# Norms by logarithm and exponential on ScalarE, and expert table units moved from the first down product to the second gate and up product

## What is computed

```
y = x * rsqrt(mean(x * x) + 1e-6) * gain
```

## Time and profile before

| | |
|---|---|
| runs of the kernel | 3768.0, 3773.07 and 3775.91 us, median 3773.07 |
| the profiled execution | 3776.11 us, span 3774.3 us |
| mean granted TensorE clock | 0.971 of full speed |
| TensorE matrix products busy | 3540.8 us, 94% of the span |
| VectorE busy | 2212.3 us, 59% |
| ScalarE busy | 1366.3 us, 36% |
| GpSimd busy | 1836.6 us, 49% |

### The profile page before, as it was taken

How to read it: one execution, slowest core, us unless ns; L and a number is a source line. 1 busy time by engine, 2 the same in 40 slices (tenths; PEclk the granted TensorE clock), 3 DMA queues, 4 the chain that set the end, 5 groups by cost and what they waited for, 6 DMA issues and landing times. The chain is left out here.

```text
span 3774.3 us, 49804 instructions
## 1 busy us (share of the span) xinstructions
PE 3540.8 (94%) x17547; PEld 2997.5 (79%) x17547; DVE 2212.3 (59%) x4244; ACT 1366.3 (36%) x1915; POOL 1836.6 (49%) x909
## 2 busy tenths in 40 slices
PE   8999987899999899996888999989999999999999
PEld 5777766777787688773677667769999999999999
DVE  4553255422234355216675565458999998677776
ACT  4332234233344322222323245423335454444443
POOL 5666423223344254332333311335566666788886
PEclk9999988999999999997999999999999999999999
DMA  6997854444557266331324211586448999899996
GB/s 244 382 375 262 301 165 149 130 137 151 160 192 245 67 201 190 105 107 39 125 88 133 88 57 62 184 302 224 158 162 295 347 344 348 317 397 389 384 383 237
DMA packets 458130, 813.81 MB, mean 216 GB/s; under 512 B 31544, under 2 KB 308984, under 8 KB 455322
## 3 DMA queue, kind: packets, MB, share of 16 engines
q1 hardware_dynamic: 278416, 436.07, 34.4%
q10 hardware_dynamic: 142666, 241.11, 18.2%
q0 software_dynamic: 36864, 134.23, 9.4%
HBM read 682.84 MB, written 195.56 MB: 233 GB/s over the span
## 5 line engine op out<-in xcount | busy, mean ns | idle before, releaser
L536 POOL TENSOR_TENSOR weights_lo<-weights_raw,weights_hi 128x1024 fp32r<-128x1024 f32 x649 | 1591.6, 2457 | 1866.1 <-ACT weights_hi L1211 1743.8
L612 PE MATMUL bank<-operand_hi,weights_hi 128*128 128x512 f32 (+1 forms) x2856 | 1095.3, 384 | 65.4 <-DVE operand_lo L1904 24.2
L614 PE MATMUL bank<-operand_hi,weights_lo 128*128 128x512 f32 (+1 forms) x2856 | 1065.1, 373 | 0.0
L613 PE MATMUL bank<-operand_lo,weights_hi 128*128 128x512 f32 (+1 forms) x2856 | 1064.3, 373 | 0.0
L1211 ACT ACTIVATE weights_hi<-weights_raw 128x1024 fp32r<-128x1024 f32 x649 | 682.3, 1056 | 827.5 <-PE bank L614 649.0
L612 PEld LDWEIGHTS bank<-operand_hi,weights_hi 128*128 128x128 f32 x2856 | 542.4, 190 | 158.7 <-DVE operand_lo L1904 30.4
L613 PEld LDWEIGHTS bank<-operand_lo,weights_hi 128*128 128x128 f32 x2856 | 542.7, 190 | 75.2 <-issue 6.4
L614 PEld LDWEIGHTS bank<-operand_hi,weights_lo 128*128 128x128 f32 x2856 | 540.8, 189 | 75.1
L612 PE MATMUL bank<-expert_hi,weights_hi 128*128 128x384 f32 x1024 | 344.1, 336 | 0.0
L613 PE MATMUL bank<-expert_lo,weights_hi 128*128 128x384 f32 x1024 | 344.0, 336 | 0.0
L614 PE MATMUL bank<-expert_hi,weights_lo 128*128 128x384 f32 x1024 | 344.0, 336 | 0.0
(11 more groups left out here) (397 smaller groups left out, 4979.2 us busy)
## 6 DMA issues: line engine op xcount, KB each, us to landing
weights_raw<-in_w_ffn_gu SPq DMA_DIRECT2D x132, 512.0 KB, 5.8
expert_table_v<-in_w_peer_out SPq DMA_DIRECT2D x120, 512.0 KB, 5.4
weights_raw<-in_w_peer_ahead SPq DMA_DIRECT2D x120, 512.0 KB, 3.8
weights_raw<-in_w_peer_out SPq DMA_DIRECT2D x120, 512.0 KB, 6.4
expert_table_u<-expert_turned ACTq DMA_DIRECT2D x288, 128.0 KB, 4.6
expert_rows<-in_w_peer_ahead ACTq DMA_DIRECT2D x64, 512.0 KB, 6.7
peer_gates<-gate_stage SPq DMA_DIRECT2D x24, 1024.0 KB, 8.6
expert_gates<-peer_gates ACTq DMA_DIRECT2D x16, 1536.0 KB, 12.5
```

The costliest lines, as they stand in the source:

```text
L536: pool.tensor_tensor(LO[:, slot, :], RAW[:, slot, :], HI[:, slot, :].bitcast(F32), ALU.subtract).then_inc(sem("lo_ready"), 1)
L612: pe.matmul(out, wh, hi(k), start=(k == 0), stop=False)
L613: pe.matmul(out, wh, lo(k), start=False, stop=False)
L614: ins = pe.matmul(out, wl, hi(k), start=False, stop=(k == kc - 1))
```

## The change

A norm's first step and its reciprocal leave VectorE. ScalarE computes Ln of the scaled sum plus epsilon straight from the bank, then Exp of minus one half of it; where asked, it first loads the one table set that has both functions, before its waits. VectorE only waits. Six of the `d1` units stay (two each at blocks 1, 2 and 3), eighteen move to `f2`, which turns two per pair and saves them in the same pair, behind the SiLU. The wait for the `d1` stores moves behind the norm. Two norms get other destination buffers.

```
-TABLE = {"f1": range(0, 54), "d1": range(54, 78), "f2": range(78, 96), "q": range(96, 128)}
+TABLE = {"f1": range(0, 54), "d1": range(54, 60), "f2": range(60, 96), "q": range(96, 128)}
+DOWN_TURNS = [0, 2, 2, 2, 0, 0, 0, 0]
...
-            def root(width):
+            def root(width, denom=D, bank=4, out=None, read=None, table=True):
                 n["sum"] += 1
+                if table:
+                    act.preload_act_table_set("natural_log_exp_and_others")
+                act.wait_ge(sem("square_used"), n["square"])
+                act.activation(RT[:, 0:width], BANK[bank][:, 0:width], ACT.Ln, bias=TINY[:], scale=1.0 / denom)\
+                    .then_inc(sem("sum_read"), 1)
                 act.wait_ge(sem("sum_read"), n["sum"])
-                act.activation(RT[:, 0:width], MS[:, 0:width], ACT.Sqrt).then_inc(sem("root_ready"), 1)
+                if read:
+                    act.wait_ge(sem(read[0]), read[1])
+                act.activation(RSTD[:, 0:width] if out is None else out, RT[:, 0:width], ACT.Exp, scale=-0.5)\
+                    .then_inc(sem("root_ready"), 1)
...
-                        if s == 0 and 3 <= pair <= 20:
+                        if s == 0 and mix == 2 and 3 <= pair <= 20:
                             save_rows(which)
...
-                        if s >= 2 and 2 <= pair <= 19:
-                            save_rows(which)
+                        if 2 <= pair <= 19:
+                            if mix == 2 and s >= 2:
+                                save_rows(which)
+                            elif mix == 1 and s == 1:
+                                for _ in range(2):
+                                    save_rows(which)
...
                     if name == "ffn1":
-                        for _ in range(3):
+                        for _ in range(DOWN_TURNS[m]):
                             save_rows("d1")
                     square(YT[:, m, :], TOK, "block_free", n["freed"] + m + 1)
-                    if name == "ffn1" and m == DC - 1:
-                        for i in range(2):
-                            act.wait_ge(sem(f"table_stored_d1{i}"), 64 * len(TABLE["d1"]) // 2)
...
             ffn("ffn1", n["freed"], x_squares)
             root(TOK)
+            for i in range(2):
+                act.wait_ge(sem(f"table_stored_d1{i}"), 64 * len(TABLE["d1"]) // 2)
...
-                root(TOK)
+                root(TOK, P, read=("piece_made", n["f"] + h) if h else None, table=h == 0)
...
                 if c % 2:
-                    root(TOK)
+                    root(TOK, 64, out=MS[:] if c == 3 else None, table=c == 1)
...
             for c in range(8):
-                root(TOK)
+                root(TOK, 64, table=c == 0)
...
-            def rstd(pieces, denom, width, bank=4, out=None):
-                n["square"] += pieces
+            def rstd():
                 n["sum"] += 1
-                dve.wait_ge(sem("square_used"), n["square"])
-                dve.tensor_scalar(MS[:, 0:width], BANK[bank][:, 0:width], 1.0 / denom, EPS, ALU.mult, ALU.add)\
-                    .then_inc(sem("sum_read"), 1)
                 dve.wait_ge(sem("root_ready"), n["sum"])
-                link(dve.reciprocal(RSTD[:, 0:width] if out is None else out, RT[:, 0:width]))
...
-                which, each = ("f2", 1) if k else ("f1", 3)
+                which, each = ("f2", 2) if k else ("f1", 3)
...
                     for m in range(DC):
-                        for t in range(3 * m, 3 * m + 3):
+                        for t in range(sum(DOWN_TURNS[:m]), sum(DOWN_TURNS[:m + 1])):
                             turn_rows("d1", t)
                         copy_blocks(YT, 1, FC, first=m, scaled=True)
```

More of the change, by code:

```diff
@@ L169, in late_at @@
     return range(count * u // units, count * (u + 1) // units) if u < units else range(0)
-TABLE = {"f1": range(0, 54), "d1": range(54, 78), "f2": range(78, 96), "q": range(96, 128)}
+TABLE = {"f1": range(0, 54), "d1": range(54, 60), "f2": range(60, 96), "q": range(96, 128)}
+DOWN_TURNS = [0, 2, 2, 2, 0, 0, 0, 0]
+assert sum(DOWN_TURNS) == len(TABLE["d1"])
 WOUT_TURNS = 9
@@ L236, in program @@
         ms_at = fixed[0]
-        MS = place("mean_square", [P, TOK])
-        RT = place("root", [P, TOK])
+        MS = place("second_reciprocal_root", [P, TOK])
+        RT = place("log_mean_square", [P, TOK])
         RSTD = place("reciprocal_root", [P, TOK])
@@ L247, in program @@
         RSUM = place("exp_sum_reciprocal", [P, 2])
+        TINY = place("norm_epsilon", [P, 1])
         A0 = fixed[0]
@@ L1411, in ffn @@
                             square(CT[:, c, :], NMEM, "ctx_loaded", 16)
-                        root(NMEM)
+                        root(NMEM, bank=5, out=MS[:, NMEM:2 * NMEM])
                         highs(CXH, CT, DC, lambda c: MOD[:, c, 1:2])
@@ L1501, in x_squares @@
             def x_squares():
+                act.wait_ge(sem("epsilon_set"), 1)
                 for c in range(DC):
@@ L1852, in _ @@
             st = Stepper()
-            n = {"freed": 0, "square": 0, "sum": 0, "high": 0, "piece": 0, "exp": 0, "product": 0,
+            n = {"freed": 0, "sum": 0, "high": 0, "piece": 0, "exp": 0, "product": 0,
                  "gate": 0, "groups": [], "operand": 1, "made": 0}
             link = Link(dve, sem("dve_order"))
+            dve.memset(TINY[:], EPS).then_inc(sem("epsilon_set"), 1)
             def done(kc):
@@ L1981, in two_pairs @@
                             turn(i, p, 0)
-                            if each > 1:
-                                turn(i, p, 1)
+                            turn(i, p, 1)
                         dve.wait_ge(sem("pe_steps"), s0 + UNIT * ((2 * p + 1) * mix + 1) + 4 * mix * UNIT * i)
@@ L1992, in two_pairs @@
                                           ALU.subtract).then_inc(sem("hidden_ready"), 1)
-                        if table and each > 1:
+                        if table and each == 3:
                             turn(i, p, 2)
@@ L2013, in ffn @@
                     for m in range(DC):
-                        for t in range(3 * m, 3 * m + 3):
+                        for t in range(sum(DOWN_TURNS[:m]), sum(DOWN_TURNS[:m + 1])):
                             turn_rows("d1", t)
                         copy_blocks(YT, 1, FC, first=m, scaled=True)
-                    rstd(DC, D, TOK)
+                    rstd()
                 else:
                     copy_blocks(YT, 2, FC, scaled=True)
-                    n["square"] += 1
-                    rstd(DC, D, NMEM, 5, MS[:, NMEM:2 * NMEM])
+                    rstd()
                     normed(CT, CT, CXH, CXL, NMEM, lambda c: COEF[:, 1, c:c + 1], lambda c: MOD[:, c, 1:2],
@@ L2285, in _ @@
             for pair in range(2):
-                rstd(2, 64, TOK)
+                rstd()
+                by = MS if pair else RSTD
                 for j in range(2):
@@ L2307, in transformed @@
                 free(dve.tensor_tensor(KHAT[:, o, m, :], done(TT)[:], norm[:], ALU.mult))
-            for o, norm in enumerate((RSTD, RT)):
+            for o, norm in enumerate((RSTD, MS)):
                 dve.wait_ge(sem("abs_used"), 8 * (o + 1))
```

18 lines of the change are left out of this document (9 added, 9 removed).

## The result

The changed kernel took **3732.5 us** (median of 4 runs, 3727.2 to 3734.6) against 3774.5 for the kernel before on the same chip (3768.0 to 3778.4): ratio 0.989, 95% interval 0.987 to 0.991. The forecast was 3725 in a range of 3713 to 3740. The profiled execution took 3727.16 us, span 3725.3; before, 3776.11 and 3774.3: 49 us less, where the sum had said 48. By medians it is 42 us less, 6 short of the sum and 7.5 us above the time forecast, inside the range: the profiled execution was the fastest of the changed kernel's four.

What follows compares the result with a forecast made beforehand. The prediction took TensorE, at 94% of the span, as the bound. Gains from its shortened waits summed to 47.75, say 48 us, turning the median of 3773.07 us into 3725, range 3713 to 3740.

Steps and rivals of the forecast that it cites:

- First down product: First down product and its norm: three terms together take 15.6 us off the start of the next stage.
- (1): Start of the first down product: TensorE's wait for a low weight part goes, as block 0 saves none; 2.7 us.
- (2): End of the first down product: without units there, the last block is copied out sooner and the norm starts earlier; 8.2 us.
- (3): Norm behind the first down product: 3.35 us from the norm itself, plus its table load now beside the last sum; 4.7 us.
- Terms given back: Rival, chance 0.12: after a shortened wait VectorE or GpSimd is the next bound; gain 30 to 38 us, time 3740.
- Heads, output product, second projections: Exposed norms at the four heads, behind the output product and before the second block's projections: gains 3.9, 3.35 and 3.35 us.
- The first term: Behind the second down product: the norm's root ends earlier despite a new exposed table load; gain 1.4 us.
- The second term: Context keys: Ln frees the second sum's bank, which TensorE waited for, earlier; gain 2.0 us.
- Query and key norms: Eight norms in the second block: TensorE's work, not the norm chain, sets the swaps' pace at 7.35 us; gain 15.5 us.
- two loads per norm: Rival, chance 0.07: the preload doesn't hold, each Exp gets its own load, some 3 us in the query loop; time 3739.
- The moved units: 18 more units in the second gate and up product fit beside its matrix work; cost 0, bounds 0 to 9 us.
- the buffer loop: Second gate and up product: stores, load, landing and transpose must fit in a pair's 11.1 us, so landings may take 7.5.

Runs made afterwards that it cites:

- experiment 1: The change's two halves, each alone on the kernel before: new norms with old table-unit shares 3740.4 us; old norms with new shares 3757.5 us.
- experiment 6: Changed kernel with the six units left in the first down product turned beside its last two blocks, not blocks 1 to 3: 3734.9 us.
- experiment 7: Changed kernel with the weight split done ahead of the last square in the first down product, not after the norm's root: 3727.8 us.
- the combined kernel: Changed kernel with table loads off the path, weight split ahead of the last square behind both down products, five DMA issues behind the second's root: 3726.0 us.
- the repeat: The changed kernel itself, unaltered, measured and profiled once more beside the combined kernel: 3726.5 us.
- Experiment 5: Changed kernel with 18 more table units moved from the first to the second gate and up product, three per pair there: 3785.9 us.
- experiment 4: Changed kernel without the named table set loaded ahead of its norms: 3731.5 us.
- experiment 3: Changed kernel with the last norm's table load ahead of ScalarE's DMA issues and no load where the set is still held: 3725.9 us.

## Why the forecast held, point by point

**The sum as a whole (47.75; 47.4 and 45.2 by stages, 42 by medians).** The mechanism is the one forecast: every exposed norm got shorter, the units hide, the swaps go at TensorE's pace. That the sum met the first profile to half a microsecond is in part luck. It had no term for the clock, which gave 5 to 7 us, and terms that were too large made up for it. The clock stood in the forecast's range, not in its sum.

**First down product (forecast 15.6, measured 14.5).** TensorE's waits say what each term was. (1) The 2.70 us at block 0 are gone, as said; experiment 1 brings them back (2.64). (2) The wait for the last square went from 7.85 to 0.59, 7.3 us where the term said 8.2; experiment 6 brings it back by itself (7.3). (3) The wait behind the norm went from 10.56 to 7.95, 2.6 us where the term said 4.7. What was missed is the 2 us of the slow scaling: with it removed (experiment 7) the wait is 5.90, 4.7 less, and the stage gains 16.3. The three waits together give 12.6, and the last 2 of the 14.5 came with the clock (0.980 over the stage against 0.938). "Terms given back" had VectorE or GpSimd as the next bound, and named this product's 8.2 as a term at risk, not its norm.

**Heads, output product, second projections (3.9, 3.35, 3.35).** Measured as shorter waits of TensorE: 10.23 to 6.17 at the heads (the stage gained 4.0), 8.60 to 5.30, 7.68 to 4.38 (3.3 each). The norm's arithmetic was right to a tenth. The output product's stage gained 4.1 and 2.6 in the two profiles with the same wait in both; the difference is the clock, 0.980 and 0.961.

**Behind the second down product and the context keys (1.4 + 2.0).** Together 2.9 and 2.3 in the two profiles. The first term did not arrive: the first scaling began 1.37 us earlier after the last square (6.44 us, before 7.81), as forecast, but two scalings now ran beside GpSimd's two subtractions, where before one did, and VectorE reached the filters' first argument 13.8 us after that square, before 13.6.

```profile
1659.74 5.45 POOL L539 TENSOR_TENSOR weights_lo<-weights_raw,weights_hi 128x1024 fp32r<-128x1024 f32 x2 [10.18 <-ACT weights_hi L1214]
1660.06 0.48 DVE L2270 TENSOR_SCALAR context_k<-bank,vectors 128x256 f32<-128x256 f32 x1
1660.45 2.48 DVE L1951 SCALAR_TENSOR_TENSOR branch_out<-branch_out,vectors,reciprocal_root 128x512 f32<-128x512 f32 x1
...
1662.97 2.78 DVE L1953 SCALAR_TENSOR_TENSOR residual<-branch_out,residual 128x512 f32<-128x512 f32 x1
```

The rival called this place the likeliest, by the 2.98 us of one such product; the sum should have gone by that row. That these scalings are what TensorE's time there hangs on is read from the rows; the combined kernel, which shortened both, also moved DMA issues. The second term did arrive: TensorE's wait for the second sum's bank fell from 2.80 to 0.87 us.

**Query and key norms (15.5).** The seven periods gave 15.8 (14.85 forecast), with swaps 7.2 us apart where the text had 7.35, and the first swap 0.6 and 0.1 us (0.65). The swap at 2125.56 in the earlier trace rows is the first of the eight, not the second. TensorE's work sets the period, as forecast, and even two loads per norm don't reach it, which the rival had priced at 3 us.

**Last norm (2.65).** The wait went from 12.00 to 9.53 us, and 9.59 in the repeat.

**The moved units (0).** Right: TensorE never waited for them in the second product. Landings, at 6.5 us median, were above the 6.0 taken and under the 7.5 of the buffer loop; a few went over it, to 8.4, and TensorE waited for none of them. Experiment 5 agrees with the loop from its other side, up to what it leaves open on the DMA engines. The transfers were only moved: DMA share 0.83 there and 0.51 in the down product, before 0.54 and 0.85.

**What was not in the sum.** Against the forecast the first down product lacks 1.1 us, the second down product with the context keys 0.5 and 1.1, the neighbourhood attention 1.6 (at a clock of 0.66 behind the last swap; 0.3 in the repeat) and the experts, which the change doesn't touch, 1.1 and 2.3. On the other side stand the second gate and up product with 1.6 and 2.3 us more, the dilated attention with 0.9 and 0.8, and the eight swaps with 0.9. The experts' part is not explained. All that the runs show is that it goes with the norms: the two profiles with the old norms have 928.0 and 928.1 us there, the other ten 929.1 to 931.8, at clocks of 0.998 against 0.996 to 0.998.

**The page weighed.** The Trainium skill, ScalarE: Activation LUTs, What ACT_TABLE_LOAD costs, has a drain of some 1380 ns at each switch. In the changed kernel's rows Ln starts 1.29 us after the load's start (467.77 to 469.06), an exposed load cost 1.25 to 1.28 us of TensorE's wait in experiment 4, and taking one away gave 1.2 in experiment 3. The measurement decides: no drain is seen here.

## What to carry to other kernels

A reciprocal of a root by Ln and Exp from one named table set costs two short activations where scaling, root and VectorE's reciprocal cost 4.8 us; it pays where the chain of the norm is the longest wait, and most where it is the period of a loop. Background work with few load buffers belongs into a long product, and not beside the last block ahead of a norm (7.3 us in experiment 6): check stores plus load plus landing plus turn, over the number of buffers, against the time that a pair of products gives. A wait can cost more than itself where the clock falls with it (12.6 us of waits in the first down product were worth 14.5), and a sum of waits should carry that as a term of its own. After shortening such a chain, look at what now runs beside its first VectorE operations.

## What the runs showed of the hardware

Some VectorE operations wait for GpSimd's subtraction instead of sharing with it. A scaling takes 0.69 us alone, 2.71 us when begun 0.31 us after the start of a subtraction of 2.47 us, and 0.69 again when the subtraction was moved away (experiment 7). The operation ended 0.55 us after the subtraction, somewhat less than its own 0.69: it did next to nothing until then. In the whole trace of the changed kernel all 20 operations of L1951, L1953 and L2002 (operands in SBUF, no bank) that began within such a subtraction ended 0.55 us after it, whenever they had begun. The Trainium skill, SBUF — State Buffer, SBUF: two separate sides, calls the port pair of the two engines an exclusive lock, held for a whole instruction; the rows agree.

It is not every operation. The cast of one operand in SBUF (L2000) was held too: all 13 that began within a subtraction ended 0.28 to 0.32 us after it, the longest after 2.62 us, where 0.43 is usual. Operations with an operand in a bank were not (L1990, 0.69 us in all 44), nor were the transposes (L1960, 1.25 us at the most).

```profile
178.39 2.40 POOL L539 TENSOR_TENSOR weights_lo<-weights_raw,weights_hi 128x1024 fp32r<-128x1024 f32 x1 [0.60 <-ACT weights_hi L1214]
178.45 2.62 DVE L2000 CAST hidden_hi<-gate_silu 128x512 f32 x1
```

The time of one execution scatters by some 10 us. Between the two profiles of the changed kernel, 6.1 us apart, 3.9 arise in one stage, the first gate and up product. TensorE waits there for modulation rows in up to nine small pieces, 1.7 to 11.8 us in all over the profiles (331.7 us up to its end with 1.7, 343.3 with 11.8), but the clock has a part in it too: the two profiles of the changed kernel have nearly the same waits, 7.2 and 7.5, and clocks of 0.995 and 0.985. What decides either from run to run was not tried.

The granted clock behind a short stretch of waits is not a constant of the kernel. Over the 20 us after the same eight swaps it was 0.66 in three of the twelve profiles, with the stage at 180.5 to 180.6 us, 0.74 in five (179.0 to 179.3), 0.83 in one (179.0) and 0.91 in three (176.6 to 177.5). That is worth up to 4 us, and nothing in the kernels compared explains which of them gets which; the changed kernel itself had 0.66 and 0.74. A gain or a price of 1 to 4 us can so be given back in a stage that the change doesn't touch.
